# The second and third attention: order of transposes and value products on TensorE, and their PSUM banks

## What is computed

```python
# second attention (window_gqa): 16 query heads, 4 key/value heads, head size 64;
# 256 latent keys in a window of 128, 256 context keys, and a sink logit
s_w = einsum(q, k_w) * scale;  s_w = where(valid, s_w, NEG_INF)
s_c = einsum(q, k_c) * scale
p = softmax(concatenate([s_w, s_c, sink]))
o = einsum(p_w, v_w) + einsum(p_c, v_c)          # then @ w_o

# third attention: three kinds of heads, 6 dilated + 6 block-gated + 4 memory = 16,
# head size 64, 256 keys each; the kernel expresses the kinds by a bias on the logits
p = softmax(s + bias)
o = einsum(p, v)                                  # then rms_norm per kind, @ w_out
```

## Time and profile before

| | us |
|---|---|
| median of 3 runs | 2818.67 |
| range of the runs | 2818.17 to 2819.75 |
| time of the profiled execution | 2818.46 |
| its span | 2816.7 |
| TensorE matmul busy | 2711.8 (96%) |
| VectorE busy | 1858.6 (66%) |
| ScalarE busy | 1221.1 (43%) |
| GpSimd busy | 161.4 (6%) |

### The profile page before, as it was taken

One profiled execution on the slowest core, in us unless ns is written; L12 is line 12 of the kernel. 1 busy time (PEld: TensorE's weight loads), 2 busy tenths in 40 slices (PEclk: granted clock), 3 DMA queues, 4 the chain that ended last, 5 costly groups with the idle time before them and its releaser, 6 DMA issues.

```text
span 2816.7 us, 46627 instructions
## 1 busy us (share of the span) xinstructions
PE 2711.8 (96%) x16042; PEld 2329.1 (83%) x16042; DVE 1858.6 (66%) x3356; ACT 1221.1 (43%) x1999; POOL 161.4 (6%) x126
## 2 busy tenths in 40 slices
PE   6999999989999999999997899998999999999999
PEld 4778887747888888888885699986998999888888
DVE  6877346486877437776348665556698777777765
ACT  5222235374422224222245554466444555555543
POOL 0000013100100001000011100000250000000000
PEclk9999999999999999999999999999999999999999
DMA  7554322212454433544232155642465555676754
GB/s 276 194 192 174 105 98 83 75 61 75 176 182 179 142 105 130 191 180 167 102 105 68 61 180 187 223 143 83 161 224 187 175 177 173 230 241 241 242 196 140
DMA packets 144846, 445.34 MB, mean 158 GB/s; under 512 B 16080, under 2 KB 44880, under 8 KB 144208
## 3 DMA queue, kind: packets, MB, share of 16 engines
q1 hardware_dynamic: 112896, 409.51, 42.3%
q10 hardware_dynamic: 31824, 34.09, 3.4%
HBM read 428.33 MB, written 15.20 MB: 157 GB/s over the span
## 4 chain that ended last, share of the span: by engine, by line
PE 88%; DVE 5%; ACT 3%; issue 2%; DMA 1%; POOL 0%; SPq 0%; ACTq 0%; DVEq 0%
PE bank L2040 23%; PE bank L2042 22%; PE bank L2041 22%; PE bank L2563 12%; PE bank L2532 2%; PE bank L2426 1%; DVE w_lo L1220 1%; PE bank L2268 1%; PE bank L2331 1%; PE bank L2407 1%; PE bank L2090 1%; DMA ada_start<-w_stream_dram 1%; ACT w_hi L668 1%; DVE part L1375 1%; ACT probs L874 0%
## 5 line engine op out<-in xcount | busy, mean ns | idle before, releaser
L2040 PE MATMUL bank<-H,w_hi 128*128 128x256 f32 (+1 forms) x3344 | 1104.9, 330 | 13.0 <-DVE H L1256 6.7
L2042 PE MATMUL bank<-H,w_lo 128*128 128x256 f32 (+1 forms) x3344 | 1080.3, 323 | 0.0
L2041 PE MATMUL bank<-H,w_hi 128*128 128x256 f32 (+1 forms) x3344 | 1080.0, 323 | 0.0
L1220 DVE TENSOR_TENSOR w_lo<-raw,w_hi 128x1024 fp32r<-128x1024 f32 x605 | 739.0, 1228 | 456.4 <-ACT w_hi L668 455.7
L668 ACT ACTIVATE w_hi<-raw 128x1024 fp32r<-128x1024 f32 x628 | 659.8, 1051 | 231.6 <-PE bank L2042 192.4
L2040 PEld LDWEIGHTS bank<-H,w_hi 128*128 128x128 f32 x3344 | 638.8, 191 | 84.5 <-issue 26.3
L2041 PEld LDWEIGHTS bank<-H,w_hi 128*128 128x128 f32 x3344 | 639.4, 191 | 51.9 <-issue 4.3
L2042 PEld LDWEIGHTS bank<-H,w_lo 128*128 128x128 f32 x3344 | 638.7, 191 | 49.1
L1375 DVE SCALAR_TENSOR_TENSOR part<-ada_side,cs,part 128x512 f32<-128x512 f32 x420 | 288.5, 747 | 1.7 <-DMA ada_side<-w_stream_dram 1.7
L2040 PE MATMUL bank<-act_hi,w_hi 128*128 128x512 f32 (+1 forms) x770 | 267.4, 347 | 0.0
L2042 PE MATMUL bank<-act_hi,w_lo 128*128 128x512 f32 (+1 forms) x770 | 266.9, 347 | 0.0
(11 more groups left out here) (236 smaller groups left out, 2399.2 us busy)
## 6 DMA issues: line engine op xcount, KB each, us to landing
raw<-w_stream_dram SPq DMA_DIRECT2D x636, 512.0 KB, 3.4
ada_side<-w_stream_dram SPq DMA_DIRECT2D x120, 512.0 KB, 4.0
gelu_scratch<-gelu ACTq DMA_DIRECT2D x108, 128.0 KB, 3.5
gelu_in<-gelu_scratch ACTq DMA_DIRECT2D x108, 128.0 KB, 3.4
ada_start<-w_stream_dram SPq DMA_DIRECT2D x16, 512.0 KB, 14.7
bias<-bias_in_dram ACTq DMA_DIRECT2D x1, 3072.0 KB, 10.0
X<-x_in_dram SPq DMA_DIRECT2D x1, 2048.0 KB, 8.4
mem<-mem_in_dram SPq DMA_DIRECT2D x1, 1024.0 KB, 5.4
```

The source lines that it names most:

```text
L1220: nc.vector.tensor_tensor(w_lo[:, s, :], raw[:, s, :], w_hi[:, s, :].bitcast(F32), ALU.subtract).then_inc(lo_ready, 1)
L2040: nc.tensor.matmul(to, w_hi[:, s, cut], hi, start=first, stop=False, skip_group_check=True)
L2041: nc.tensor.matmul(to, w_hi[:, s, cut], lo, start=False, stop=False, skip_group_check=True)
L2042: return nc.tensor.matmul(to, w_lo[:, s, cut], hi, start=False, stop=last, skip_group_check=True)
```

## The change

The value bank alternates between 6 and 7 in `pair_b` too. `values` handles one unit at a time: the same matmuls with 128 columns in place of 256, twice as many of them, and `pv_ready` is still raised once for a pair. It waits for the `pT_ready` of its own unit, and with its first unit for the reader of pair p-2 in both stages. In each step TensorE now does `scores(u)`, `transposes(u-2)`, `values(u-3)`. ScalarE's and VectorE's programs are not changed, except that they read the alternating bank.

```diff
         def value_bank(pair, p):
 
-            return bank[6 + p % 2 if pair == "pair_c" else 6]
+            return bank[6 + p % 2 if pair != "pair_a" else 6]
...
-                def values(p):
-                    pe.wait_ge(of(pair, "pT_ready"), per * (p + 1))
-
-                    if pair == "pair_b":
-                        if p >= 1:
-                            pe.wait_ge(of(pair, "ol_ready"), p)
-                    elif p >= 2:
-                        pe.wait_ge(of(pair, "o_ready"), p - 1)
+                def values(u):
+                    p, q = units[u]
+                    pe.wait_ge(of(pair, "pT_ready"), u + 1)
+                    if p >= 2 and q == 0:
+                        pe.wait_ge(of(pair, "ol_ready" if pair == "pair_b" else "o_ready"), p - 1)
                     to = value_bank(pair, p)
+                    cut = slice(q * P, (q + 1) * P)
                     nk = 4 if pair == "pair_b" else 2
                     for k in range(nk):
                         for c in range(2):
                             t = pT[:, p % 2, c * D:c * D + nk * NT].rearrange("p (k q) -> p k q", k=nk)
                             at = (p // 2) * HEAD if pair == "pair_b" else (2 * p + c) * HEAD
                             v = (V if pair == "pair_b" else Vc)[:, k, at:at + HEAD]
-                            ins = nc.tensor.matmul(to[HEAD * c:HEAD * (c + 1), 0:NT], v, t[:, k, :], start=k == 0,
+                            ins = nc.tensor.matmul(to[HEAD * c:HEAD * (c + 1), cut], v, t[:, k, cut], start=k == 0,
                                                    stop=k == nk - 1)
-                    ins.then_inc(of(pair, "pv_ready"), 1)
+                    if q == per - 1:
+                        ins.then_inc(of(pair, "pv_ready"), 1)
 
                 for u in range(len(units) + LAG + 1):
                     if u < len(units):
                         scores(u)
-                    if u > LAG and (u - LAG) % per == 0:
-                        values((u - LAG) // per - 1)
                     if LAG <= u < len(units) + LAG:
                         transposes(u - LAG)
+                    if u > LAG:
+                        values(u - LAG - 1)
```

## The result

| | before | changed |
|---|---|---|
| median, us | 2819.18 (6 runs) | 2802.9 (6 runs) |
| range of the runs | 2818.17 to 2820.89 | 2801.39 to 2806.18 |
| span of the profiled execution | 2816.7 | 2800.7 |
| `pair_b`, first scores to first product of `out_b` | 69.97 | 56.72 |
| `pair_c`, first scores to first sums of `og_c` | 38.86 | 36.31 |

The ratio is 0.9943 with an interval of 0.9933 to 0.9954: the change takes 16.3 us away, where 15.4 were forecast. The two stages give 13.25 and 2.55 of the 16.0 by which the span fell, so the two stages together account for all but 0.2 of it. Outside of them two unchanged stretches differ as well and nearly cancel: `pair_b` starts 1.77 us later than before, and what follows `pair_c` is 1.96 us shorter.

The account below looks back on a forecast made before the run. Loops through several engines, containing the whole value product, were taken to set the pace, with no engine full in the attentions' steady parts. Gains of 11.5 in `pair_b` and 3.9 in `pair_c`, 15.4 us, gave 2803.1 us; range 2799.5 to 2811.0.

Parts of the forecast that it names:

- The unit's value product: TensorE's time for one unit's value product: 1.09 us in `pair_b` (1.03 to 2.01), 0.61 in `pair_c` (0.58 to 1.07).
- The pace of `pair_b`: Steady part of `pair_b`: 6.34 us a pair from TensorE's own work, above a loop of 6.23, instead of 7.44.
- The sum for `pair_b`: Whole `pair_b`: 2.1 us gained up to unit 4, 4.4 over four pairs, 5.0 at the end; 11.5 in all.
- Its share of 2.5: End of `pair_b`: about 2.5 us of the 11.5 gained come from full clock instead of mostly 1.2 GHz.
- The sum for `pair_c`: Whole `pair_c`: 0.9 us at the start, 2.1 over four pairs, 0.5 and 0.4 at the end; 3.9 in all.
- The pace of 3.68: Steady part of `pair_c`: 3.68 us a pair instead of 4.21, from TensorE's 3.66 and an estimated loop of 3.69.
- About 0.7 is added because the clock is still low there: Start of `pair_c`: 0.7 us added to the 4.9 of eight steps, putting unit 4 at 1902.3 instead of 1903.20.
- Not abreast: Rival, chance 0.07: short value products don't run two abreast, a unit costs 2.01 and 1.07 us; 2824.3 us.
- Weight loads: Rival, chance 0.07: weight loads show unhidden between value products, 0.17 us per record pair, units of 1.53 and 0.83; 2812.9 us.
- The clock falls at the end: Rival, chance 0.12: the clock drops at the end of `pair_b` as before, costing 0.8 + 0.8 + 0.9 us; 2805.6 us.
- ScalarE keeps the pace: Rival, chance 0.07: in `pair_c` ScalarE's `o_out` waits for the later value product, a pair stays at 4.21; 2807.0 us.
- Nothing changes: Rival, chance 0.03: TensorE's standing moves from value products to transposes, which still wait for weighing and copies; 2818 us.

Follow-up runs that it names:

- e4: Changed kernel, but whole pairs of 256 columns in the value products, behind the transposes in every second step, two banks in both stages; 2811.89 us.
- e2: Kernel before, with only the second output bank added in `pair_b`, order unchanged; 2814.53 us, ratio 0.9988.
- e3: Changed kernel, but with one output bank in `pair_b`, the new order kept; 2825.63 us, ratio 1.0023.
- e10: Changed kernel with the new order in `pair_c` alone; `pair_b` in the old order with bank 6 alone; 2815.8 us, ratio 0.9987.
- e7: Changed kernel with the new order in `pair_b` alone, `pair_c` in the old order; 2809.46 us, ratio 0.9960.
- e11: Changed kernel, plus unit-wise values behind transposes in the first attention, each pair's first unit held back one step; 2799.23 us, ratio 0.9930.
- e12: The same program as e11, measured again against the kernel before; 2798.15 us, ratio 0.9927.
- e1: Changed kernel with a unit's value products reordered: all of head 0, then all of head 1; 2809.05 us, ratio 0.9966.
- e6: Changed kernel with a unit's value product ahead of the next unit's transposes instead of behind them; 2810.82 us, ratio 0.9970.
- e9: Changed kernel with a unit's value products ordered head 0 twice, head 1 twice, and so on; 2803.84 us, ratio 0.9944.

## Why the prediction was right

The mechanism was as forecast, and the time, 2803.1, was met within the noise (2802.9). That it was met to 0.2 us is luck: `pair_b` gave 1.75 more than its sum and `pair_c` 1.35 less. About 0.9 of the one and all of the other are the clock at the start of the stage, which no row of the kernel before foretells. Part by part:

- *The unit's value product.* Forecast 1.09 in `pair_b` and 0.61 in `pair_c`, measured 1.03 and 0.59. The low end of the range holds: eight times 0.107 and 0.17. Weights at 0.113 a record on the full array told too much; that two loads of half the columns each cost less is a likely reason, but no run separates it.
- *The pace of `pair_b`.* Forecast 6.34, set by TensorE, with a loop of 6.23 just below; measured 6.21, TensorE without a gap. With the measured 1.03 the two are 2 x 3.11 = 6.22 and 6.17, so still TensorE, by less. e4, which puts the whole value product into that loop, lands on the sum of its terms, 7.02.
- *The two parts together.* The text counted the bank and the order as one gain. e2 and e3 show what it didn't work out: the bank alone is worth 0.12% in time, and the order alone is a loss of 0.23%, since a value product that comes later also frees its bank later. The loss is all in `pair_b`: e10, which differs from e3 only in the order there, is at 0.9987, so that order with one bank costs 0.36%. Without the 1.5 of clock a pair of e3 would still take 8.7, against 7.44.
- *The sum for `pair_b`.* 2.1 up to unit 4, 4.4 on, 5.0 at the end were forecast; 3.2, 4.9 and 5.1 were measured, 13.25 for 11.5. At the start the scores ahead of unit 1's transposes ran at full clock (1.13 us where they had taken 2.00); in e7, where they didn't, `pair_b` takes 57.61, which is 12.4 less than before. This too can differ for one program: 57.63 in e11 and 56.71 in e12. The clock at the end was 1.00, as assumed. Its share of 2.5 holds against this one profile of the kernel before; in e10, with the same order and bank in `pair_b`, the clock fell less far (0.76 from 1576.00 to 1581.00, and 1.00 after that) and the end took 16.56 and not 17.95, so that against e10 the share is only about 1.1.
- *The sum for `pair_c`.* 3.9 forecast, 2.55 in the pair of profiles that stand first, 4.0 and 4.1 between profiles of like clock. The pace of 3.68 was met, and set by the loop through weighing as estimated (3.69), with TensorE's 3.62 just below. The mechanism was right, and the missing 1.4 is the clock of the first 10 us, 0.50 for 0.83: the term mis-sized is "About 0.7 is added because the clock is still low there", taken over from the profile before. Unit 4 was forecast 0.9 earlier after the start of the stage and came 0.5 later (13.59 for 13.06); the other two terms, 2.1 for the four pairs and 0.9 for the end, were met with 2.13 and 0.95.
- *The rivals.* "Not abreast" fell: 16 records in 1.09. e1 shows that its danger was real, though smaller: with another order of the same products over half of the gain of `pair_b` is gone. "Weight loads" fell with the 1.03: by the Trainium skill's 81 ns a matmul (TensorE: Matmul & The Clock Gate, "Back-to-back issue gap"), counted for each record, it would have been 1.47, an estimate. The section says nothing of matmuls that leave two records or stand side by side, and the trace disagrees for them: they come two every (1.09 - 0.23) / 8 = 0.107. "The clock falls at the end" fell, and so did "ScalarE keeps the pace": no wait for a value product shows before the last units. "Nothing changes" fell with the two paces. What e6 adds is that the place behind the transposes is no side matter: the prediction had it behind them, but it named the copies only as a wait that costs nothing, and the expectation of e6 took the place for indifferent.

## What to carry to other kernels

Draw every loop that goes through an operation before moving it, also the short one between two engines: splitting the value product took it out of the loop through scores and maxima, and only its place behind the transposes kept it out of the one through the copies. An operation that is moved back also gives its buffer back later, so a second buffer may be worth little in the old order and decide the sign in the new one. Before a change of this kind is judged from one pair of profiles, compare the granted clock of the stretches; 1.5 us of 4 were that here. And take more than one profile of the kernel before, too.

## What was unexpected in the hardware

- Products for different halves of the array's columns run abreast also when they aren't direct neighbours: two products of one head ahead of two of the other cost 0.04 a unit (e9), four ahead of four cost 0.48 (e1), and two ahead of two in `pair_c` nothing (0.59 in e1 and e9).
- After a wait of 2.38 us in each pair (e3) the clock is 0.55 for the next 3.6 us, which costs 1.5 us more than the wait itself; with a wait of 1.08 in each pair it is 1.00. In the kernel before, the clock of 0.63 at the end of `pair_b` likewise begins behind a wait of 2.14:

```profile
1573.11 3.00 PE L2426 MATMUL bank<-pT,V 128*64 128x256 f32 x16 [2.14 <-DVE H L1643]
```

- The first 10 us of `pair_c` ran at 0.50 in one execution of a program and at 0.61 in another (e11, e12), and `pair_c` took 36.29 and 35.30 us.
